# Mixer gates of a four-layer network: seven block products for each slab of gate weights, gates made with tanh

## The reference, cut to what matters

```python
def token_mixer(h, positions, w_in, ..., gate_w, gate_b, branch_w, out_w):
    proj = h @ w_in                       # 1024 -> retention, forget and latent attention inputs
    ya = retention(...)                   # three branches of width 512
    yb = blocked_causal_attention(..., f_cum)
    yc = blocked_causal_attention(...)
    gates = jax.nn.sigmoid((h @ gate_w + gate_b))      # 256 x 1024 @ 1024 x 3072
    gates = gates.reshape(B, S, N_BRANCH, D)
    merged = gates[:, :, 0] * (ya @ branch_w[0])
    merged = merged + gates[:, :, 1] * (yb @ branch_w[1])
    merged = merged + gates[:, :, 2] * (yc @ branch_w[2])
    return merged @ out_w
```

## Time and profile before

| What | Value |
|---|---|
| median of 3 runs | 2345.03 us (2344.78 to 2348.25) |
| the profiled execution: its own time | 2346.33 us |
| its span | 2344.4 us |
| granted TensorE clock, mean | 0.997 |
| busy: PE / PEld / DVE / ACT / POOL | 2301.5 / 1336.4 / 917.8 / 440.8 / 75.5 us |
| mixer of layer 0, mixer of layer 1 | about 832 to 1110 us, about 1587 to 1865 us of the span |

### The profile page before, as it was taken

The page is one execution under the profiler, slowest core; times in us unless marked ns, Lnnn a source line. Parts: engine busy times, 40 slices in busy tenths (PEclk is TensorE's granted clock), DMA queues, the critical chain, the costliest instruction groups (busy, mean ns, idle before and its releaser), DMA issues.

```text
span 2344.4 us, 23511 instructions
## 1 busy us (share of the span) xinstructions
PE 2301.5 (98%) x9874; PEld 1336.4 (57%) x9874; DVE 917.8 (39%) x1799; ACT 440.8 (19%) x995; POOL 75.5 (3%) x130
## 2 busy tenths in 40 slices
PE   8999999999999999999999999999999999999998
PEld 6568548875586448787434333335878643333343
DVE  3557656667676444462211121122346221111112
ACT  3410003267100021220111111111122021111111
POOL 2000000010100000000000000000000000000000
PEclk9999999999999999999999999999999999999999
DMA  7389625354797433246899999994325699999997
GB/s 288 116 307 397 249 84 188 140 193 172 273 419 289 147 117 133 94 167 264 359 428 427 428 428 427 428 418 178 110 90 219 245 376 428 428 426 428 428 428 294
DMA packets 58007, 671.52 MB, mean 286 GB/s; under 512 B 7376, under 2 KB 7664, under 8 KB 18592
## 3 DMA queue, kind: packets, MB, share of 16 engines
q1 hardware_dynamic: 50736, 649.45, 68.2%
q0 software_dynamic: 7152, 20.43, 2.6%
HBM read 666.59 MB, written 3.26 MB: 286 GB/s over the span
## 4 chain that ended last, share of the span: by engine, by line
PE 86%; DMA 10%; DVE 3%; issue 0%; ACT 0%; SPq 0%; POOL 0%; DVEq 0%; POOLq 0%; ACTq 0%
PE ps L101 84%; DMA ring<-in_exp_w 8%; DVE arena L114 1%; DVE arena L117 1%; PE ps L335 1%; DMA arena<-ssm_rows 1%; PE ps L2550 1%; DMA ring<-in_ada_w 0%; DMA ring<-in_attn_w_in 0%; PE ps L611 0%; DVE arena L110 0%; PE ps L1752 0%; DVE X L117 0%; PE ps L1203 0%; POOL small L117 0%
## 5 line engine op out<-in xcount | busy, mean ns | idle before, releaser
L101 PE MATMUL ps<-arena 128*64 128x512 f32 (+6 forms) x3412 | 867.2, 495 | 15.3 <-DMA arena<-in_exp_w 5.5
L101 PEld LDWEIGHTS ps<-arena 128*128 128x128 f32 (+2 forms) x3412 | 382.8, 162 | 460.9 <-issue 433.0
L101 PE MATMUL ps<-XTGB,ring 128*128 128x256 f32 x2608 | 578.7, 380 | 0.0
L101 PEld LDWEIGHTS ps<-XTGB,ring 128*128 128x128 f32 x2608 | 490.6, 190 | 77.5 <-issue 11.3
L101 PE MATMUL ps<-ring,arena 128*64 128x512 f32 (+1 forms) x1636 | 442.2, 596 | 6.6 <-DMA ring<-in_exp_w 6.6
L101 PEld LDWEIGHTS ps<-ring,arena 128*64 128x64 f32 (+1 forms) x1636 | 159.7, 149 | 261.5 <-issue 258.8
L122 DVE COPY arena<-ps 128x512 f32<-128x512 f32 (+4 forms) x139 | 67.4, 504 | 507.2 <-PE ps L101 375.3
L101 PE MATMUL ps<-ring,XTGB 128*128 128x512 f32 (+3 forms) x568 | 226.8, 557 | 1.0 <-DMA ring<-in_attn_w_in 0.8
L121 ACT COPY arena<-ps 128x512 f32<-128x512 f32 (+3 forms) x185 | 85.1, 479 | 645.3 <-PE ps L101 313.6
L105 ACT ACTIVATE arena<-ps 128x512 f32<-128x512 f32 (+1 forms) x81 | 47.6, 594 | 663.9 <-PE ps L101 663.9
L101 PEld LDWEIGHTS ps<-ring,XTGB 128*128 128x128 f32 x568 | 106.1, 192 | 114.0 <-issue 108.5
(11 more groups left out here) (146 smaller groups left out, 900.6 us busy)
## 6 DMA issues: line engine op xcount, KB each, us to landing
arena<-in_exp_w SPq DMA_DIRECT2D x90, 2048.0 KB, 29.0
ring<-in_exp_w SPq DMA_DIRECT2D x76, 2048.0 KB, 27.9
ring<-in_mlp_w SPq DMA_DIRECT2D x25, 2048.0 KB, 9.2
ring<-in_ada_w SPq DMA_DIRECT2D x20, 2048.0 KB, 9.8
XTGB<-in_exp_w SPq DMA_DIRECT2D x18, 2048.0 KB, 34.3
ring<-in_ssm_w_in SPq DMA_DIRECT2D x12, 2048.0 KB, 8.1
ring<-in_w_in SPq DMA_DIRECT2D x12, 2048.0 KB, 8.0
ring<-in_gate_w SPq DMA_DIRECT2D x12, 2048.0 KB, 7.6
```

The costliest lines, as they stand in the source:

```text
L101: return self.e.matmul(o, lhsT=lhsT, rhs=rhs, start=start, stop=stop, skip_group_check=True)
```

## The change

A slab of weights is cut in 2 x 2 blocks: contraction chunks 0 to 3 and 4 to 7, output features 0 to 255 and 256 to 511. The activations `XT` are cut in 2 x 2 as well: the same halves of the contraction, and tokens 0 to 127 and 128 to 255. Seven products of blocks (numbered 1 to 7) take the place of eight. They need four sums of blocks of the weights per slab, four sums of blocks of XT per mixer, and seven sums of products per slab.

- TensorE: gap(4s + r) makes the products in `GROUPS[r]`: (1, 6), (5, 7), (3, 4), (2,), each product 8 matmuls with 128 x 128 weights and 128 moving columns. Products 3 to 7 wait for sums.
- GpSimd: `gate_sums` makes the sums of weights, each over 128 x 1024 elements in SBUF: part 0 is S1 and S2, part 1 is a difference written over a block of the slab, part 2 (the fourth sum, written over S2) waits for the first group of its slab. S1 and S2 have two buffers, used in turn by the slabs.
- VectorE: `x_sums` makes the sums of XT (four of 128 x 512 elements) between the two ropes; its gaps add the products (256 columns each) instead of `+ 1` and the reciprocal; gap(9) and gap(17) are moved ahead.
- ScalarE: a copy of product 1, and four tanh per slab, done in the gaps of the next slab. The gate is now tanh(x/2), the branch products are multiplied by (gate + 1), and the factor 0.5 is applied to the output product.
- GpSimd's three DMA issues now wait for ("rqk", l, 0).

```diff
+        GROUPS = ((1, 6), (5, 7), (3, 4), (2,))
+
+        def factors(p, w, S):
+            x = {1: XT[:, 0:4, 0:P], 2: XT[:, 4:8, 0:P], 3: XT[:, 4:8, P:T], 4: bT[4], 5: bT[1], 6: bT[2], 7: bT[3]}[p]
+            y = {1: w[:, 0:4, 0:T], 2: w[:, 4:8, 0:T], 3: S[2], 4: w[:, 4:8, T:2 * T], 5: S[1], 6: S[2],
+                 7: w[:, 0:4, T:2 * T]}[p]
+            return x, y
+
+        def x_sums(v, l, nn):
+            v.wait_ge(at("XT", nn, 0), at("XT", nn, 1))
+            k = v.then_inc(v.tt(bT[1], XT[:, 0:4, P:T], XT[:, 0:4, 0:P], ALU.subtract), ("bT", l))
+            v.then_inc(v.tt(bT[3], XT[:, 4:8, P:T], XT[:, 0:4, P:T], ALU.subtract), ("bT", l))
+            v.wait_ge(k)
+            k = v.then_inc(v.tt(bT[2], XT[:, 4:8, P:T], bT[1], ALU.subtract), ("bT", l))
+            v.wait_ge(k)
+            v.then_inc(v.tt(bT[4], XT[:, 4:8, 0:P], bT[2], ALU.subtract), ("bT", l))
+
+        def gate_sums(e, l, s, part):
+            w = weights(("g", l, s))
+            S = bS[s % 2]
+            if part == 0:
+                e.wait_ge(at("w", ("g", l, s)), at("g", l, 4 * s - 6) if s >= 2 else None)
+                k = e.then_inc(e.tt(S[1], w[:, 0:4, T:2 * T], w[:, 4:8, T:2 * T], ALU.add), ("bS", l, s, 1))
+                e.wait_ge(k)
+                e.then_inc(e.tt(S[2], S[1], w[:, 0:4, 0:T], ALU.subtract), ("bS", l, s, 2))
+            elif part == 1:
+                e.wait_ge(at("bS", l, s, 1))
+                e.then_inc(e.tt(w[:, 0:4, T:2 * T], w[:, 0:4, 0:T], w[:, 0:4, T:2 * T], ALU.subtract), ("bS", l, s, 3))
+            else:
+                e.wait_ge(at("g", l, 4 * s))
+                e.then_inc(e.tt(S[2], w[:, 4:8, 0:T], S[2], ALU.subtract), ("bS", l, s, 4))
...
 (mix_pe, gap)
-                    for c in range(8):
-                        ins = pe.mm(ps[:, 0:T], w[:, c, (q % 4) * P:(q % 4 + 1) * P], XT[:, c, :], c == 0, c == 7)
+                    for k, p in enumerate(GROUPS[r]):
+                        x, y = factors(p, w, bS[s % 2])
+                        if p >= 3:
+                            pe.wait_ge(at("bT", l), at("bS", l, s, {3: 4, 4: 2, 5: 1, 6: 2, 7: 3}[p]))
+                        for f in range(2):
+                            for c in range(4):
+                                ins = pe.mm(ps[:, k * T + f * P:k * T + (f + 1) * P], y[:, c, f * P:(f + 1) * P], x[:, c, :],
+                                            c == 0, c == 3)
...
 (mix_act, gap)
-                    act.wait_ge(at("g", l, q), at("ngb", l))
-                    act.then_inc(act.act(gT[:, q, :], ps_of("g", l, q)[:, 0:T], ACT.Exp, bias=gb[:, q:q + 1], scale=-1.0),
-                                 ("gexp", l, q), ("read", "g", l, q))
+                    if r == 0:
+                        act.wait_ge(at("g", l, q))
+                        act.then_inc(act.cp(gate_blocks(l, s)[0], product(l, q, 0)), ("P1", l, s), ("read", "g", l, q))
+                    elif s:
+                        for j in ((0, 1), (2,), (3,))[r - 1]:
+                            gate_out(4 * s - 4 + j)
+
+            def gate_out(q):
+                act.wait_ge(at("gsum", l, q // 4), at("hgb", l))
+                act.then_inc(act.act(gT[:, q, :], gT[:, q, :], ACT.Tanh, bias=gb[:, q:q + 1], scale=0.5), ("gate", l, q))
...
 (mix_dve, gap)
-                    v.wait_ge(at("gexp", l, q))
-                    k = v.then_inc(v.ts(gT[:, q, :], gT[:, q, :], 1.0, None, ALU.add))
-                    v.wait_ge(k)
-                    v.then_inc(v.recip(gT[:, q, :], gT[:, q, :]), ("gate", l, q))
+                    if r == 0:
+                        v.wait_ge(at("P1", l, s))
+                        v.then_inc(v.tt(c12, product(l, q, 1), c11, ALU.add), ("U2", l, s), ("read", "g", l, q))
+                    elif r == 1:
+                        v.wait_ge(at("U2", l, s))
+                        k = v.then_inc(v.tt(c21, product(l, q, 1), c12, ALU.add), ("read", "g", l, q))
+                        v.then_inc(v.tt(c12, product(l, q, 0), c12, ALU.add), ("U4", l, s), ("read", "g", l, q))
+                        v.wait_ge(k)
+                        v.then_inc(v.tt(c22, product(l, q, 0), c21, ALU.add), ("U3", l, s), ("read", "g", l, q))
+                    elif r == 2:
+                        v.wait_ge(at("U3", l, s), at("U4", l, s))
+                        v.then_inc(v.tt(c12, product(l, q, 0), c12, ALU.add), ("gsum", l, s), ("read", "g", l, q))
+                        v.then_inc(v.tt(c21, product(l, q, 1), c21, ALU.add), ("gsum", l, s), ("read", "g", l, q))
+                    else:
+                        v.then_inc(v.tt(c11, product(l, q, 0), c11, ALU.add), ("gsum", l, s), ("read", "g", l, q))
...
 (mix_dve: branch products, output product)
-                    k = v.then_inc(v.tt(t_, ps, g_, ALU.mult), ("read", "br", l, br, fp))
+                    k = v.then_inc(v.stt(t_, g_, 1.0, ps, ALU.add, ALU.mult), ("read", "br", l, br, fp))
...
 (mix_pool)
-            pool.wait_ge(at("rqk", l, 1))
+            pool.wait_ge(at("rqk", l, 0))
...
+            sums((0, 0), (0, 1), (0, 2), (1, 0), (1, 1))
             rstd(pool, rs8, at("rvar", l), ("rrstd", l))
+            sums((1, 2), (2, 0), (2, 1))
             pool.wait_ge(at("yT", l, 0))
...
             rstd(pool, rs_q, at("mq var", l), ("mq rstd", l))
             rstd(pool, rs_k, at("mkv var", l), ("mkv rstd", l))
+            sums((2, 2))
+            for s in range(3, 6):
+                sums((s, 0), (s, 1), (s, 2))
             rms_pool(pool, nn + 1)
```

More of the change, by code:

```diff
@@ L1679, in build @@
         gq, sq_q, sq_k = arena.get(384), arena.get(256), arena.get(128)
+        att_end = arena.pos
         arena.pos = after_misc
@@ L1690, in build @@
         m_bufs = att_bufs()
+        arena.pos = max(att_end, arena.pos)
+        bT = [None] + [arena.get(4, P) for _ in range(4)]
+        bS = [[None] + [arena.get(4, T) for _ in range(2)] for _ in range(2)]
+        assert arena.pos <= ASZ - D
         arena.pos = work
@@ L1708, in fill, with gate_blocks, product @@
             return ("gate", n) if 0 <= n < 24 else (None, 0)
+        GROUPS = ((1, 6), (5, 7), (3, 4), (2,))
[26 more added lines that the diff above has]
+                e.then_inc(e.tt(S[2], w[:, 4:8, 0:T], S[2], ALU.subtract), ("bS", l, s, 4))
+        def gate_blocks(l, s):
+            g = gT[:, 4 * s:4 * s + 4, :]
+            return g[:, 0:2, 0:P], g[:, 0:2, P:T], g[:, 2:4, 0:P], g[:, 2:4, P:T]
+        def product(l, q, k):
+            return ps_of("g", l, q)[:, k * T:(k + 1) * T].rearrange("p (f t) -> p f t", f=2)
         def mix_sp(sp, l):
@@ L1816, in gap @@
                 if what == "gate":
-                    s = ("g", l, q // 4)
-                    w = weights(s)
+                    s, r = divmod(q, 4)
+                    slab_ = ("g", l, s)
+                    w = weights(slab_)
                     ps = bank(pe, "g", l, q)
-                    pe.wait_ge(at("w", s))
-                    for c in range(8):
-                        ins = pe.mm(ps[:, 0:T], w[:, c, (q % 4) * P:(q % 4 + 1) * P], XT[:, c, :], c == 0, c == 7)
-                    pe.then_inc(ins, ("g", l, q), *([("free", s)] if q % 4 == 3 else []))
+                    pe.wait_ge(at("w", slab_))
+                    for k, p in enumerate(GROUPS[r]):
[6 more added lines that the diff above has]
+                                            c == 0, c == 3)
+                    pe.then_inc(ins, ("g", l, q), *([("free", slab_)] if r == 3 else []))
             for t in range(2):
@@ L2078, in mix_act @@
                     causal_act(act, l, 2, i - 2, "apply", m_bufs)
-            gap(24)
-            gap(25)
+            for q in range(20, 24):
+                gate_out(q)
             x_turned(act, l, 0, 0)
@@ L2095, in gap @@
                 if what == "gate":
[L2096 to L2099 removed]
+                    s, r = divmod(q, 4)
+                    c11, c12, c21, c22 = gate_blocks(l, s)
+                    v.wait_ge(at("g", l, q))
+                    if r == 0:
[13 more added lines that the diff above has]
+                        v.then_inc(v.tt(c11, product(l, q, 0), c11, ALU.add), ("gsum", l, s), ("read", "g", l, q))
             v.wait_ge(at("gate_b", l), at("XT", nn, 1))
[L2102 removed]
+            v.then_inc(v.ts(gb, gb, 0.5, None, ALU.mult), ("hgb", l))
             k = None
@@ L2105, in mix_dve @@
             for t in range(2):
+                if t:
+                    x_sums(v, l, nn)
                 v.wait_ge(at("rqk", l, t), k)
@@ L2137, in mix_dve @@
                 v.then_inc(v.tt(rqk[:, t, :], rqk[:, t, :], rg[:, t, :], ALU.mult), ("ry", l, t))
-            for n in range(5, 9):
+            for n in range(5, 10):
                 gap(n)
@@ L2173, in mix_dve @@
             turned(v, ("lat", l), 1, latT, 3, ("latT", l))
-            gap(9)
             for i in range(6):
@@ L2185, in mix_dve @@
             gap(16)
+            gap(17)
             k = None
@@ L2204, in mix_dve @@
                 turned(v, ("kpT", l), t, kpT, 1, ("mla ready", l))
```

(8 more changed lines are left out.)

4 lines of the change are left out of this document (3 added, 1 removed).

## The result

The changed kernel takes 2366.45 us (median of 4 runs, 2364.65 to 2369.93); the kernel before, on the same chip, takes 2346.32. The ratio is 1.0087 (95% interval 1.0076 to 1.0099): slower by 0.9%. The forecast was 2338 us with a range up to 2357, so the time lies outside the range, beyond even the rival that called for the full price of contention (2359). The profiled execution took 2364.65 us, span 2362.8, against 2346.33 and 2344.4 before: 18.3 us more. One run in this document, of the version with shorter sums, lasted 7927.5 us at a mean granted clock of 0.34, and is left out of that version's ratio; its cause is open.

What follows compares the result with a forecast made beforehand. TensorE's matmuls were taken to bound each mixer. Matmuls -15.7, new waits +2.6 and contention +5.8 gave -7.3 us; from the 2345.03 us median the forecast was 2338 us, range 2330 to 2357.

Steps and rivals of the forecast that it cites:

- the rival that called for the full price of contention: Every VectorE instruction on SBUF operands waits for a whole GpSimd sum: +14.3 us, 2359 us; chance 0.18.
- VectorE against GpSimd: Prediction's section on VectorE instructions waiting beside GpSimd's weight sums in each mixer; 2.9 us a mixer taken.
- VectorE keeps its turn: VectorE instructions in a row let no GpSimd sum between them; waits of 2.9 us a mixer instead of 13.7.
- the three places: Turn of lat, second branch's head loop, third branch's q ropes: tight VectorE chains beside GpSimd sums, 2.9 us a mixer.
- the sum had 5.8: Forecast's term for TensorE waits from VectorE and GpSimd contention, both mixers: 2.9 us each.
- The slack at lat: Time to spare before TensorE wants lat: 4.8 us, less one 1.28 us table load on ScalarE, leaving 3.5.
- the rival's 6.1 us for this place: Wait at lat if each of four VectorE instructions meets a 2.4 us sum, after 3.5 us of slack.
- In the loop: Second branch, normalise of head 2 after group 12: wait 4.3 us at one sum per instruction, otherwise 2.0.
- at the ropes: Third branch's q ropes beside slab 5's sums: wait about 3.3 us if three sums are met, 0.9 if two.
- The pitch: Time per 128-column gate matmul on TensorE: 0.1117 us, the weight load just keeping up.
- the -15.7: Gain from fewer, smaller gate matmuls on TensorE: 1.31 us a slab, 15.7 us over 12 slabs.
- The waits at gap(6) and gap(11): New TensorE waits without contention: 0.6 us for a slab's fourth sum, 0.7 for a head's normalise; 2.6 in all.

## Why the prediction was wrong

**The step that failed** is the choice under "VectorE against GpSimd": "Sum: 13.7 us a mixer if each instruction meets one, 2.9 if VectorE keeps its turn. I take 2.9", with the reason that four VectorE instructions with no idle time between them "leave GpSimd no room to slip in". They do leave room. Each of lat's four instructions waited for a sum, 9.83 us for 1.41. The new waits at the three places are 3.28 + 3.68 + 3.38 = 10.3 us a mixer, 20.7 in both, where the sum had 5.8. The row I leaned on could not carry this: it was taken with GpSimd silent, so it showed how close VectorE's instructions stand, not who gets the ports between two of them. The rival's mechanism ("every VectorE instruction on SBUF operands waits for a whole sum") is the one that holds, but for reductions and reciprocals, which lost nothing, and moved bursts (-34 us) and split sums (-30 us) show it from two sides.

**A term that was not in the sum** is the clock. Behind waits of some 3 us TensorE runs at 1.2 GHz for a while, 5.9 us lost in mixer 0 and 4.6 in mixer 1 by the rows above; filling the waits gave 8.1 us back in two mixers. This is why the time lies above 2359, although the port waits (10.3 a mixer) are smaller than that rival's 13.7. Any forecast of new waits on TensorE needed this term beside it.

**The slack at lat** was taken as 3.5 us because of one more table load in the chain. The timeline of ACT, changed kernel, has the additional one elsewhere:

```profile
945.90 1.28 ACT L105 ACT_TABLE_LOAD   x1
```

The extra load falls in time in which ScalarE had nothing to do (its next instruction is at 952.74), and the chain has one load, at 952.96, as in the earlier trace rows. Real slack: lat could have been ready at 958.74 + 1.41 = 960.15, and was wanted at 964.94 + 0.49 = 965.43, 5.3 us. With it the rival's 6.1 us for this place becomes 9.83 - 1.41 - 5.3 = 3.1, against 3.28 measured. In the loop 4.3 was asked by the same rival and 3.68 measured, at the ropes 3.3 and 3.38. The last agreement says little: the prediction gives no working for its 3.3 and 0.9, and the only slack that it shows there, 1014.30 to 1015.09, does not lead to them.

**What held.** The pitch: 32 gate records from 895.48 to 899.06 are 0.112 us each, as forecast, with weight loads keeping up, and the two mixers without sums, 7.2 us shorter each, confirm the -15.7 to within half a microsecond. A sum costs 2.35 to 2.46 us for 2.4. The waits at gap(6) and gap(11) are 0.53 and 0.46 for 0.6 and 0.7. The tanh, the PSUM sums and the four sums of XT cost nothing. A mixer's change of time is kept in full: the expert weights are issued 8.8 us later than in the earlier trace rows, and the stage behind is as long as it was.

```profile
1059.75 40.42 SPq L247 DMA_DIRECT2D ring<-in_exp_w  x4
```

With measured terms the sum reads -15.7 (matmuls) + 2.0 (gap(6), gap(11)) + 20.7 (ports) + 12.3 (clock and restarts, what is left of both mixers: 6.8 and 5.5) = +19.3, for +19.4 measured over the two mixers. That this closes proves nothing, as the last term is the rest; by the rows 10.5 of its 12.3 are clock. Outside them 1.0 us less was measured, since the first projection of mixer 0 starts 1.5 us earlier, ahead of all that was changed.

## What to carry to other kernels

Before work is given to an idle GpSimd, list, in the chains that TensorE waits for, VectorE's two-input instructions with both inputs in SBUF and its multiplies from SBUF to SBUF (reductions, reciprocals and what has an operand in PSUM were not slowed here): each one beside a stream of GpSimd sums costs up to one whole GpSimd instruction, however short it is itself and however closely VectorE's instructions follow each other. So place the bursts where VectorE has slack or works from PSUM, or cut them into short instructions (2.4 to 0.75 us was enough here), or leave them on VectorE if it has room; all three turned 0.9% slower into 0.4 to 0.7% faster. And price a new wait on TensorE higher than its length: at the three places with some 3 us of wait the matmuls behind lost another 1.4 to 2.8 us at half the clock in mixer 0, and 0 to 2.9 in mixer 1.

## What the runs showed that was not expected

- The two engines go strictly in turn: 4 VectorE instructions of 0.35 us and 4 GpSimd ones of 2.4 take 9.83 us; GpSimd itself is hardly delayed (2.33 to 2.52 us beside them).
- A 128x2 multiply of 0.17 us took 0.97 beside a sum, while the reductions, the reciprocals (1753 ns each in the run with the sums alone) and the instructions with an operand in PSUM kept their time.
- In mixer 0 TensorE's granted clock fell to 0.5 behind waits of 3.28 and 3.68 us, and not behind those of 0.5 us; in mixer 1 it stayed at 1.0 behind the same 3.28. With the waits filled its mean was 1.00 through both mixers.
- The turns ahead of mixer 1 have an idle time of 4.0 us before, 4.5 after, and 4.30 + 5.10 with three kinds of idle-work added far ahead of it, with nothing in the trace that ends it.
